# Drain of the last SSD layer: TensorE's second z half between the turns of the inputs, VectorE's splits and masks ahead of the second exponents

## What is computed

```
z, xbc, dt = split(h @ w_in)            # z: 2048 columns, x: 2048, B and C: 8 groups x 128
xbc = silu(dwconv(xbc))
cum = cumsum(dt * a)                    # running sums, per head and direction
decay = exp(where(lower, cum[l] - cum[s], -inf))
y = ((C @ B^T) * decay) @ (x * dt) + (C * exp(cum)) @ h_state     # both directions
y = y + x * d_skip
out = rms_norm(y * silu(z), norm_g) @ w_out
```

## Time and profile before

| what | value |
|---|---|
| median of 3 runs | 1536.99 us (1532.41 to 1537.48) |
| profiled execution | 1531.61 us |
| span of the profile | 1530.3 us |
| TensorE busy in the span | 1455.0 us (95%) |
| VectorE, ScalarE, GpSimd busy | 1132.9, 705.9, 329.0 us |
| mean granted TensorE clock | 0.988 |
| the drain of layer 3, up to the scan | about 1449.5 to 1479 us of the span |

### The profile page before, as it was taken

One profiled execution on the slowest core, in us unless ns is written; L12 is line 12 of the kernel. 1 busy time (PEld: TensorE's weight loads), 2 busy tenths in 40 slices (PEclk: granted clock), 3 DMA queues, 4 the chain that ended last, 5 costly groups with the idle time before them and its releaser, 6 DMA issues.

```text
span 1530.3 us, 22697 instructions
## 1 busy us (share of the span) xinstructions
PE 1455.0 (95%) x8557; PEld 1205.2 (79%) x8557; DVE 1132.9 (74%) x1694; ACT 705.9 (46%) x1259; POOL 329.0 (21%) x379
## 2 busy tenths in 40 slices
PE   5899999999999999999899999999999999999987
PEld 3787888888877889886678887787888889888865
DVE  0688999999996385867658555646438999999996
ACT  1554554545454253455545322323324565555552
POOL 1042344344451012001000000000001234434340
PEclk9999999999999999999999999999999999999999
DMA  9245535564453413315332436444341444434443
GB/s 325 78 139 168 149 111 167 153 192 133 121 161 130 129 45 87 122 33 174 115 120 88 137 116 195 137 130 165 100 127 29 116 111 129 120 111 115 130 130 122
DMA packets 169421, 197.38 MB, mean 129 GB/s; under 512 B 9696, under 2 KB 151648, under 8 KB 169312
## 3 DMA queue, kind: packets, MB, share of 16 engines
q1 hardware_dynamic: 158480, 163.08, 34.5%
q0 software_dynamic: 9296, 30.19, 7.5%
q10 hardware_dynamic: 1536, 2.67, 0.5%
HBM read 194.59 MB, written 1.31 MB: 128 GB/s over the span
## 4 chain that ended last, share of the span: by engine, by line
PE 45%; DVE 36%; issue 8%; ACT 7%; DMA 2%; SPq 2%; POOL 1%; DVEq 0%; ACTq 0%; POOLq 0%
PE ps L437 12%; PE ps L438 11%; PE ps L439 11%; DVE xc L929 7%; DVE w_lo L406 5%; DVE cum_b L937 4%; ACT w_hi L397 2%; ACT Wb L792 2%; PE ps L466 2%; DVE Wb L956 2%; SPq L2486 1%; DVE Hs L974 1%; PE ps L618 1%; PE ps L1938 1%; PE ps L624 1%
## 5 line engine op out<-in xcount | busy, mean ns | idle before, releaser
L437 PE MATMUL ps<-h_hi,w_hi 128*128 128x512 f32 (+2 forms) x1088 | 412.2, 379 | 9.6 <-issue 4.9
L439 PE MATMUL ps<-h_hi,w_lo 128*128 128x512 f32 (+2 forms) x1088 | 398.6, 366 | 0.0
L438 PE MATMUL ps<-h_lo,w_hi 128*128 128x512 f32 (+2 forms) x1088 | 398.5, 366 | 0.0
L406 DVE TENSOR_TENSOR w_lo<-raw,w_hi 128x1024 fp32r<-128x1024 f32 (+1 forms) x203 | 244.4, 1236 | 112.0 <-ACT w_hi L397 110.3
L397 ACT ACTIVATE w_hi<-raw 128x1024 fp32r<-128x1024 f32 (+1 forms) x203 | 206.5, 1050 | 134.0 <-PE ps L439 114.1
L437 PEld LDWEIGHTS ps<-h_hi,w_hi 128*128 128x128 f32 (+1 forms) x1088 | 205.8, 189 | 54.3 <-issue 19.1
L439 PEld LDWEIGHTS ps<-h_hi,w_lo 128*128 128x128 f32 (+1 forms) x1088 | 205.3, 189 | 33.8
L438 PEld LDWEIGHTS ps<-h_lo,w_hi 128*128 128x128 f32 (+1 forms) x1088 | 205.9, 189 | 30.8
L929 DVE SCALAR_TENSOR_TENSOR xc<-ps,gp,xc 128x508 f32<-128x508 f32 (+1 forms) x224 | 162.7, 727 | 17.9 <-ACT xc L761 12.0
L439 PE MATMUL ps<-w_hi,ylo 128*128 128x512 f32 x376 | 147.1, 391 | 0.0
L1136 POOL DMA_DIRECT2D cum_b<-cum_scratch x96 | 71.8, 754 | 248.0 <-PE ps L618 168.9
(11 more groups left out here) (265 smaller groups left out, 2611.4 us busy)
## 6 DMA issues: line engine op xcount, KB each, us to landing
raw<-in_mod_w SPq DMA_DIRECT2D x80, 512.0 KB, 4.6
raw<-in_ssm_w_in SPq DMA_DIRECT2D x64, 512.0 KB, 4.9
cum_b<-cum_scratch POOLq DMA_DIRECT2D x96, 256.0 KB, 5.6
raw<-in_ssm_w_in SPq DMA_DIRECT2D x66, 256.0 KB, 4.6
raw<-in_ssm_w_out SPq DMA_DIRECT2D x32, 512.0 KB, 4.7
raw<-in_pool_w_in SPq DMA_DIRECT2D x32, 512.0 KB, 4.8
raw<-in_attn_w_in SPq DMA_DIRECT2D x20, 512.0 KB, 4.1
raw<-in_pool_w_out SPq DMA_DIRECT2D x16, 512.0 KB, 4.7
```

Of the source, the lines that this page charges most:

```text
L406: dve.tensor_tensor(lo, w_shaped(key, raw[:, r % RS, :], width), hi.bitcast(F32), ALU.subtract).then_inc(lo_done, 1)
L437: pe.matmul(o, hi_s, hi_m, start=first, stop=False)
L438: pe.matmul(o, hi_s, lo_m, start=False, stop=False)
L439: return pe.matmul(o, lo_s, hi_m, start=False, stop=last)
```

## The change

On TensorE, the second half of z moves ahead of B's transpose and of the products of C and B. On ScalarE, the exponents stay where they are, the copy of B's transpose follows the second z half, and the high parts of chunks 2 and 3 move behind the exponents. On VectorE, the split of chunk 0's weights and the masks go between `decay(0)` and `decay(1)`, the split of chunk 1 behind the gate, and the low parts of chunks 0 and 1 behind `state(1)`. No operation is added or taken away.

```
-    def pe_turn_inputs(pe, L, g):
+    def pe_turn_inputs(pe, L, g, ts=range(3)):
         s = lay[L]
-        for t in range(3):
+        for t in ts:
...
             last.then_inc(s["t1_p"], 1)
+        if 2 not in ts:
+            return
...
         ssd_project(pe, L, GRP, 4)
-        pe_turn_inputs(pe, L, g)
-        ssd_project(pe, L, GRP, 5)
+        if last_layer(L):
+
+            pe_turn_inputs(pe, L, g, (0, 1))
+            ssd_project(pe, L, GRP, 5)
+            pe_turn_inputs(pe, L, g, (2,))
+        else:
+            pe_turn_inputs(pe, L, g)
+            ssd_project(pe, L, GRP, 5)
...
-        def turned():
-            for t in range(3):
+        def turned(ts=range(3)):
+            for t in ts:
...
         if not has_in and last_layer(L):
             z_silu(g, 0)
-            turned()
+            turned((0, 1))
             z_silu(g, 1)
-            for c in range(4):
+            turned((2,))
+            for c in range(2):
                 act_yhi(act, L, c)
             cb_dt(0)
             cb_dt(1)
             exps((0, 1))
+            for c in range(2, 4):
+                act_yhi(act, L, c)
...
             y_lat(i - 2)
             decay(0)
+            dve_split(dve, L, "out", 0, 0)
+            masks()
             decay(1)
-            masks()
             gate(i - 2)
-            for c in (0, 1):
-                dve_ylo(dve, L, c)
-            for c in (0, 1):
-                dve_split(dve, L, "out", c, 0)
+            dve_split(dve, L, "out", 1, 0)
             weigh_steps(0)
             weigh_steps(1)
             state(0)
             state(1)
+            for c in (0, 1):
+                dve_ylo(dve, L, c)
             mix(0)
             mix(1)
             state(2)
```

## The result

| | before | after |
|---|---|---|
| median | 1535.6 us (22 runs, 1531.58 to 1540.92) | 1539.74 us (22 runs, 1534.75 to 1543.44) |
| profiled execution | 1531.61 us | 1539.95 us |
| span, mean granted clock | 1530.3 us, 0.988 | 1538.7 us, 0.975 |

The ratio is 1.0021, with a 95% interval from 1.0011 to 1.003: the change costs 3.2 us of 1535.6 (1.7 to 4.6). The two medians themselves lie 4.1 us apart. The median lies inside the forecast range, and the sign is as forecast. The loss is above the +2.0 of the sum, and the prediction's "a difference under 0.3% can't be told from no change" did not hold: with 22 runs on each side, a difference of 0.2% stands clear of 1.

What follows compares the result with a forecast made beforehand. The prediction took VectorE to set the pace up to the start of group 7's scan in the last layer's drain. Terms 0 + 1.6 + 0.4 gave +2.0 us; from the three-run mean of 1535.6 it forecast 1537.6, range 1531.5 to 1542.

Steps and rivals of the forecast that it cites:

- the sign: Whole kernel: slower, with the forecast case at +0.8 to +3.5 us and a chance of 0.53.
- the +2.0 of the sum: Whole kernel: 0 + 1.6 + 0.4 us, taking the profiled execution from 1531.61 to 1533.6 us.
- a difference under 0.3% can't be told from no change: Timing of the whole kernel: differences under 4.6 us would not stand clear of the runs' scatter.
- TensorE's reorder: Second z half ahead of B's transpose: 1.64 us of idling goes into the wait for the gate; cost 0.
- The gap of VectorE filled by the split: Chunk 0's split fills VectorE's 1.17 us wait for the running sums, so the states come 1.2 us earlier.
- The wait that takes its place: TensorE's chunks 0 and 1 wait for chunk 0's low part; the scan starts 1.6 us later (+0.3 to +2.3).
- GpSimd's rows are not changed by this order: GpSimd beside VectorE in the drain: its operations keep their times, so +1.6 us was taken for the low-part wait.
- A shift of the scan reaches the end one for one: Group 7's scan in the last layer's drain: any shift of its start arrives in full at the kernel's end.
- The clock: Granted clock falling in TensorE's two gathered gaps and over chunks 0 and 1: +0.4 us, from -1.7 to +1.4.
- Rival A: Clock falls twice, over chunks 0 and 1 and again in the scan: +4.7 to +5.4 us, 1540.6; chance 0.12.
- rival B: Clock's fall slides into the gaps, low part there by 1467.9: -1.7 us, at its bound -1.4, 1534.2; chance 0.13.
- C: VectorE at its shorter durations and the same single clock fall: about nothing, +0.3 us, 1535.9; chance 0.22.

Runs made afterwards that it cites:

- e2: TensorE's and ScalarE's order of the changed kernel with VectorE's order of the kernel before; ratio to before 0.9985 (0.9974 to 0.9995).
- e8: e2 timed and profiled again; ratio to before 0.9998 (0.9984 to 1.0013).
- e1: The changed kernel with VectorE's low parts of chunks 0 and 1 back behind the gate, ahead of the weighing; ratio to before 0.9989 (0.9978 to 1.0).
- e3: VectorE's order of the changed kernel with TensorE's and ScalarE's order of the kernel before; ratio to before 1.0018 (1.0005 to 1.0032).
- e4: The changed kernel with two times 24 extra transposes in TensorE's gaps ahead of the second states and chunk 0; ratio to before 1.0003 (0.9989 to 1.0016).
- e7: The kernel before with 12 extra TensorE transposes ahead of the second states and 10 ahead of chunk 0; ratio to before 0.9999 (0.9985 to 1.0014).
- e12: The changed kernel timed and profiled again; ratio to before 1.0008 (0.9996 to 1.002).
- e5: e1 with group 7's y work on VectorE moved ahead of the low parts and splits of chunks 4 and 5; ratio to before 0.9981 (0.9969 to 0.9994).
- e11: e5 timed and profiled again; ratio to before 0.9988 (0.9974 to 1.0002).
- e6: e5 with 24 extra transposes on TensorE ahead of the second states; ratio to before 1.0005 (0.9994 to 1.0017).
- e9: e7 with group 7's y work moved earlier on VectorE as in e5; ratio to before 1.0012 (1.0002 to 1.0023).
- e10: The kernel before with only group 7's y work moved earlier on VectorE, no fills; ratio to before 1.0003 (0.9991 to 1.0015).

## Why the prediction was right, and which terms were off

- **TensorE's reorder, 0:** right in the profiles (0 in e2, -0.29 us in e8); timed it is -2.3 and -0.3 us, so a small gain is possible. B's transpose starts at once behind the z half, the idling of 1.64 us goes into the wait for the gate, 3.37 us (forecast 3.8). The second z half starts at 1454.01 on the old clock, forecast 1454.3.
- **The gap of VectorE filled by the split:** right, 1.17 us of waiting for the running sums are gone, and the masks are where the forecast had them. But `state(2)` ends at 1473.23 on the old clock, 0.45 us earlier than the 1473.68 of before and not the forecast 1.2, as the rest of the gain goes into the longer operations of the next point.
- **The wait that takes its place, +1.6:** the mechanism is shown by e1 and e3. As the delay of the scan, its size was too small. Chunk 0 starts at 1470.45 on the old clock, forecast 1469.5. The failed step is "GpSimd's rows are not changed by this order": its weighted inputs took 6.80 us for 5.83 and `Wa` 3.01 for 2.22, and the split of chunk 1 and the weighing on VectorE, now beside them, grew by 0.36 and 0.74 us against the forecast. That the longer inputs alone cost nothing is seen in e1, which has them too (6.80). At full clock (e4 against e7) the scan starts 2.27 us later, 22.82 against 20.55 us from the turn of x.
- **"A shift of the scan reaches the end one for one":** wrong at full clock. Of those 2.27 us only 0.76 are left at the gate's turn (43.66 against 42.90), mostly since e7 idles 1.21 us for VectorE's y work. So the order's own cost at the end is half of the forecast +1.6. I had looked at the chain from 1473.73 on; with the clock fallen it shows no wait there.
- **The clock, +0.4:** the places were right, the fall goes from the scan into the gaps and reaches the chunks. The sum was wrong on both sides. In the chunks the half clock costs 2.44 us (e4), inside the forecast 0 to 3.1; in the scan before it cost 0.28 and not 1.7 (e7), so that there was little to win back: net +2.16, beyond the dear end of -1.7 to +1.4. Rival A's second fall, in the scan, did not come (1.95 us for the eight products), nor did rival B's early low part. The prediction also read the busy share of 7.51 us from the same ten microseconds as the fall at 120 to 130 us; ahead of that fall, which began near 124 us, TensorE had idled from about 119 to 122.5 us.

The terms as measured in the profiles: +0.76 for the order at full clock, +2.44 for the clock after, -0.28 for that of before, in all +2.92 where I had +2.0. Each stands on one profile of e4 and one of e7. The reason forecast to be the main one is thus the trigger of the loss, and the clock is the larger part of its size. That the sum came out near is in part luck: the order was 0.84 too dear and the clock 1.76 too cheap. It was luck too that the mean of three early runs, 1535.6, is the median of 22; and the range of 1531.5 to 1542 takes in the rivals A, B and C, so that the median lies inside it says little. The profile's loss goes with +3.2 us in the first timing and with +1.2 in the second (e12); how often the clock falls at which place over many executions was not measured.

The Trainium skill ("TensorE: Matmul & The Clock Gate", "Why this matters for your kernels") asks to keep long idle gaps from between bursts of matmuls. This case's trace agrees for the changed kernel, where the clock falls in such a gap and slows the chunks (8.0 us for 5.56). e5 shows a limit of the advice here: its wait for the gate is as long (3.37 us), the clock falls too, and the kernel is the fastest. The scan there still waits 0.28 us for VectorE, so the slowed work ahead of it did not set its start.

## What to carry to other kernels

When a step is moved later on a helper engine, look up everything that the main engine waits for ahead of its next work, not only the chain that the move is meant to shorten: here the split and the last state came earlier, and the low part of chunk 0, which the same chunk waits for, ended at 1470.30 on the old clock and not at 1463.54. The chunk's last input had been the split, at 1466.28. Price a fall of the clock by what waits behind the slowed work, from a run with the clock held, not by the lengthening of the matmuls. And where a kernel's executions differ by some microseconds ahead of the change, compare profiles by a distance between two events around the change.

## What the runs showed of the hardware that I had not expected

- Two engines lengthen each other: GpSimd's six multiplications took 5.82 or 6.81 us by VectorE's order alone (e2, e3). VectorE's weighing took 1.28 us behind GpSimd's work (e2), 1.70 us where GpSimd's skip term stood beside its beginning (e5), and 2.54 us beside `Wa` and the skip term (changed).
- In all seven profiles with TensorE's new order and no fill (changed, e1, e2, e5, e8, e11, e12) the clock fell in the wait ahead of the second states. In the two with 24 transposes there (e4, e6) it did not. But fills were no guarantee: in e6 and e9 it fell afterwards, in the scan, with 3.6 us for eight products that take 1.95 at full clock, and e10 kept its full clock with no fill at all.
- The same program began its drain 4.50 us later in one profiled execution than in the other (turn of x at 1458.36 in the changed kernel, 1453.86 in e12). The first had a fall of the clock between 480 and 495 us that the second had not, and that alone went with some 2.8 us.
